# Sparse-attention mixers on one Trainium2 core: both key groups of a tile side by side, with two front banks and one selected bank

## What is computed

```python
p_cmp = masked_softmax(einsum('bghsd,bngd->bghsn', qh, k_cmp), cmp_mask)     # compressed keys
o_cmp = einsum('bghsn,bngd->bghsd', p_cmp, v_cmp)
imp = einsum('bghsn,nj->bgsj', p_cmp, overlap)                               # importance of 32 blocks of 64 keys
sel_score = where(eligible, imp + FORCE_BONUS * forced, -1.0)
_, sel_idx = lax.top_k(sel_score, 8)                                         # 8 blocks for the selected branch
o_slc = softmax over the keys of the selected blocks, times their values
o_win = softmax over the last 256 keys, times their values
o = gates[0] * o_cmp + gates[1] * o_slc + gates[2] * o_win
```

## Time and profile before

| | |
|---|---|
| median of 3 runs | 3451.02 us (3449.68 to 3454.45) |
| profiled execution | 3451.55 us, its span 3449.6 us |
| mean granted TensorE clock | 0.954 |
| TensorE / VectorE / ScalarE / GpSimd busy | 93% / 42% / 29% / 31% of the span |
| first step of the mixers to last turn | 698.2 to 1766.8 us |

### The profile page before, as it was taken

How to read it: one execution, slowest core, us unless ns; L and a number is a source line. 1 busy time by engine, 2 the same in 40 slices (tenths; PEclk the granted TensorE clock), 3 DMA queues, 4 the chain that set the end, 5 groups by cost and what they waited for, 6 DMA issues and landing times. The chain is left out here.

```text
span 3449.6 us, 42933 instructions
## 1 busy us (share of the span) xinstructions
PE 3202.7 (93%) x15500; PEld 2516.8 (73%) x15500; DVE 1435.8 (42%) x2615; ACT 998.3 (29%) x1652; POOL 1078.3 (31%) x615
## 2 busy tenths in 40 slices
PE   7999998667888999999979969999999999999999
PEld 7999998644555555555548758888888878888887
DVE  3113111046656666665532133335433533354333
ACT  3012000033434444444430032232222322232221
POOL 3222221043423223222010044444344444444442
PEclk9999999658889999999999979999999999999999
DMA  5223222210101001000023342223322232333321
GB/s 172 97 96 101 97 96 81 67 55 32 64 32 64 33 32 64 32 32 7 13 105 134 117 157 94 93 94 130 102 97 97 95 126 96 97 98 122 97 97 61
DMA packets 164983, 291.21 MB, mean 84 GB/s; under 512 B 19167, under 2 KB 126559, under 8 KB 162780
## 3 DMA queue, kind: packets, MB, share of 16 engines
q1 hardware_dynamic: 160252, 272.79, 23.4%
q10 hardware_dynamic: 4608, 16.78, 1.4%
HBM read 239.01 MB, written 50.53 MB: 84 GB/s over the span
## 5 line engine op out<-in xcount | busy, mean ns | idle before, releaser
L1752 POOL TENSOR_TENSOR mlp_down_lo<-mlp_down_raw,mlp_down_hi 128x2048 fp32r<-128x2048 f32 x64 | 298.5, 4663 | 750.5 <-ACT mlp_down_hi L1791 750.5
L1872 DVE TENSOR_TENSOR mlp_y<-mlp_acc,mlp_y 128x512 f32<-128x512 f32 x512 | 344.5, 688 | 201.4 <-PE mlp_acc L1950 196.5
L1950 PE MATMUL mlp_acc<-mlp_down_hi,mlp_f_hi 128*128 128x512 f32 x1024 | 402.6, 393 | 10.6 <-DVE mlp_y L1872 10.6
L1928 PE MATMUL mlp_up<-mlp_hT_hi,mlp_up_hi 128*128 128x512 f32 x1024 | 399.6, 390 | 2.5 <-DVE mlp_hT_lo L1894 2.5
L1950 PE MATMUL mlp_acc<-mlp_down_hi,mlp_f_lo 128*128 128x512 f32 x1024 | 400.2, 391 | 0.0
L1950 PE MATMUL mlp_acc<-mlp_down_lo,mlp_f_hi 128*128 128x512 f32 x1024 | 400.1, 391 | 0.0
L1928 PE MATMUL mlp_up<-mlp_hT_hi,mlp_up_lo 128*128 128x512 f32 x1024 | 399.4, 390 | 0.0
L1928 PE MATMUL mlp_up<-mlp_hT_lo,mlp_up_hi 128*128 128x512 f32 x1024 | 399.3, 390 | 0.0
L1859 DVE TENSOR_TENSOR mlp_f<-mlp_relu 128x512 f32<-128x512 f32 x128 | 134.4, 1051 | 601.8 <-ACT mlp_relu L1798 601.8
L311 PE MATMUL proj_acc<-proj_w_hi,proj_hT_hi 128*128 128x344 f32 x1152 | 369.9, 321 | 10.9 <-issue 9.8
L311 PE MATMUL proj_acc<-proj_w_hi,proj_hT_lo 128*128 128x344 f32 x1152 | 367.9, 319 | 0.0
(11 more groups left out here) (251 smaller groups left out, 5427.0 us busy)
## 6 DMA issues: line engine op xcount, KB each, us to landing
mlp_up_raw<-in_w_up SPq DMA_DIRECT2D x64, 1024.0 KB, 5.2
mlp_down_raw<-in_w_down SPq DMA_DIRECT2D x64, 1024.0 KB, 4.8
proj_w_raw<-in_w_in SPq DMA_DIRECT2D x18, 1376.0 KB, 6.4
z_scratch<-proj_z_out SPq DMA_DIRECT2D x144, 172.0 KB, 1.9
mix_z<-z_scratch SPq DMA_DIRECT2D x16, 1548.0 KB, 6.9
proj_x_tile<-in_x ACTq DMA_DIRECT2D x16, 512.0 KB, 3.9
mixed_scratch<-mix_mixed SPq DMA_DIRECT2D x16, 512.0 KB, 2.9
out_mixed<-mixed_scratch SPq DMA_DIRECT2D x16, 512.0 KB, 4.1
```

The source lines that it names most:

```text
L1752: nc.gpsimd.tensor_tensor(dn_lo[:, b, :, :], dn_raw[:, :, :], dn_hi[:, b, :, :].bitcast(F32), ALU.subtract).then_inc(dn_lo_done, 1)
L1872: nc.vector.tensor_tensor(y[:, yb, tt, cols], acc[i % AR][:, :], y[:, yb, tt, cols], ALU.add).then_inc(added, 1)
L1928: mm = nc.tensor.matmul(up_ps[t % 2][:, :], w[:, b, k, cols], h[:, k, :], start=k == 0 and w is up_hi and h is h_hi, stop=k == KT - 1 and ...
L1950: mm = nc.tensor.matmul(acc[i % AR][:, :], a[:, b, k, tt * P:(tt + 1) * P], w[:, b, k, c * BANK:(c + 1) * BANK], start=k == 0 and a is f_h ...
```

## The change

`Plan` orders by tiles instead of by units. `front` of both groups of a tile, each followed by its own select and selected maxima, become one list, `pair(i)`: group 1 follows four steps (`LAG`) behind group 0, the steps alternating. The own work of both groups of tile i is one list too and is merged with `pair(i + 1)`, itself merged with the whole prep of tile i+2. The front bank is now two, one per group, and everything of a front that was one buffer (maxima, negated maxima, weights, sums, selection) is two; the selected bank is one, so the first "values" of a unit waits until the unit before has been lifted, turned and read by its "post". Eight banks are used before and after. No instruction's shape or count in the mixers changes, except that GpSimd clears a selection buffer of twice the size once.

```diff
@@ Plan
+LAG = 4
-        first = self.front(0) + self.select(0) + self.front(1) + self.selected_maxima(0)
-        self.steps = self.prep(0) + merge(first, self.prep(1))
-        for u in range(units):
-            i, g = divmod(u, GROUPS)
-            own = [("scores", u, SLC, 0)]
-            for j in range(1, i + 1):
-                own += [("scores", u, SLC, j), ("values", u, SLC, j - 1)]
+        self.steps = self.prep(0) + merge(self.pair(0), self.prep(1))
+        for i in range(tiles):
+            own = self.own(GROUPS * i) + self.own(GROUPS * i + 1)
             ahead = []
-            if u + 2 < units:
-                pieces = self.prep(i + 2) if i + 2 < tiles else []
-                half = len(pieces) // GROUPS
-                ahead = merge(self.front(u + 2), pieces[g * half:(g + 1) * half])
-            self.steps += own[:1]
-            if u >= 1:
-                self.steps.append(("turn", u - 1, SLC))
-            if u + 1 < units:
-                self.steps += self.select(u + 1)
-                ahead = merge(self.selected_maxima(u + 1), ahead)
-            if u >= 1:
-                self.steps.append(("post", u - 1, SLC))
-            self.steps += own[1:5] + merge(own[5:] + [("values", u, SLC, i), ("lift", u, SLC)], ahead)
-        self.steps += [("turn", units - 1, SLC), ("post", units - 1, SLC)]
+            if i + 1 < tiles:
+                ahead = merge(self.pair(i + 1), self.prep(i + 2) if i + 2 < tiles else [])
+            self.steps += merge(own, ahead)
...
+    def own(self, u):
+        tiles = list(self.key_tiles(u, SLC))
+        steps = [("scores", u, SLC, tiles[0])]
+        if u % GROUPS:
+            steps.append(("turn", u - 1, SLC))
+        steps += [("scores", u, SLC, j) for j in tiles[1:2]]
+        if u % GROUPS:
+            steps.append(("post", u - 1, SLC))
+        for j in tiles:
+            steps.append(("values", u, SLC, j))
+            steps += [("scores", u, SLC, k) for k in tiles[j + 2:j + 3]]
+        steps.append(("lift", u, SLC))
+        return steps + ([("turn", u, SLC), ("post", u, SLC)] if u % GROUPS else [])
+    def pair(self, i):
+        a, b = (self.front(u) + self.select(u) + self.selected_maxima(u) for u in (GROUPS * i, GROUPS * i + 1))
+        return a[:LAG] + [step for two in zip(a[LAG:], b) for step in two] + b[len(a) - LAG:]
@@ mixers_phase: buffers
-        selected_ps = [m.ps(f"selected{b}", [P, BANK]) for b in range(2)]
-        front_ps = m.ps("front", [P, BANK])
+        selected_ps = m.ps("selected", [P, BANK])
+        front_ps = [m.ps(f"front{b}", [P, BANK]) for b in range(2)]
@@ PE, "compressed": the front bank's wait
-                    if u >= 1:
-                        pe.wait_ge(rows_set, u)
+                    if u >= 2:
+                        pe.wait_ge(rows_set, u - 1)
@@ PE, "values": the selected bank's wait
-                        if branch == SLC and u >= 2:
-                            pe.wait_ge(selected_read, u - 1)
+                        if branch == SLC and u >= 1:
+                            pe.wait_ge(selected_read, u)
```

More of the change, by code:

```diff
@@ L720, in __init__ @@
                 self.values_n[s[1:]] = len(self.values_n)
+            elif s[0] == "post" and s[2] != SLC:
+                self.front_n[s[1:]] = len(self.front_n)
         self.probs_by = list(self.probs_n)
@@ L839, in mixers_phase @@
         chosen = m.sb("chosen", [P, NBLK])
-        selection = m.sb("selection", [P, P])
+        selection = m.sb("selection", [P, 2, P])
         weighted = m.sb("weighted", [P, HPG, HEAD])
@@ L950, in _ @@
             link(nc.gpsimd.memset(state[:, :, :], 0.0))
-            nc.gpsimd.memset(selection[:, :], 0.0).then_inc(cleared, 1)
+            nc.gpsimd.memset(selection[:, :, :], 0.0).then_inc(cleared, 1)
             pool.wait_ge(cleared, 1)
@@ L1086, in _ @@
                         act.wait_ge(turn_sum[branch], u)
-                    bank = selected_ps[u % 2] if branch == SLC else front_ps
+                    bank = selected_ps if branch == SLC else front_ps[u % 2]
                     nc.scalar.copy(lifted[branch][0:VROWS, :], bank[0:VROWS, :]).then_inc(lift_done[branch], 1)
@@ L1118, in maxima_done @@
             def maxima_done(u, branch):
-                if u >= 1:
-                    dve.wait_ge(score_sum, plan.scores_n[u - 1, branch, "row"] + 1)
-                nc.vector.tensor_scalar(neg_max[:, branch, :], top[:, branch, :], MASKED / 10, -1.0,
+                if u >= 2:
+                    dve.wait_ge(score_sum, plan.scores_n[u - 2, branch, "row"] + 1)
+                nc.vector.tensor_scalar(neg_max[:, u % 2, branch, :], top[:, u % 2, branch, :], MASKED / 10, -1.0,
                                         ALU.max, ALU.mult).then_inc(max_ready[branch], 1)
@@ L1227, in _ @@
                         dve.wait_ge(turn_sum[branch], u + 1)
-                    out = (selected_ps[u % 2] if branch == SLC else front_ps)[:, 0:HPG * VCOLS[branch]]\
+                    out = (selected_ps if branch == SLC else front_ps[u % 2])[:, 0:HPG * VCOLS[branch]]\
                         .rearrange("p (h c) -> p h c", h=HPG)
@@ L1261, in _ @@
                     else:
-                        read, count = (selected_read, u + 1) if branch == SLC else (front_read, 2 * u + 2)
+                        read, count = (selected_read, u + 1) if branch == SLC else (front_read, plan.front_n[u, WIN] + 1)
                         link(nc.vector.scalar_tensor_tensor(out=den[:, 1, :], in0=out[:, :, HEAD], scalar=1e-30,
@@ L1371, in _ @@
                         mm = nc.tensor.transpose(score_ps[n % 2][0:1, h * P:(h + 1) * P],
-                                                 neg_max[:, branch, h:h + 1], ident[:, :])
+                                                 neg_max[:, u % 2, branch, h:h + 1], ident[:, :])
                     mm.then_inc(score_sum, 1)
@@ L1417, in _ @@
                     if branch == CMP:
-                        out = front_ps[:, 0:HPG * VCOLS[CMP]].rearrange("p (h c) -> p h c", h=HPG)
+                        out = front_ps[u % 2][:, 0:HPG * VCOLS[CMP]].rearrange("p (h c) -> p h c", h=HPG)
                         for h in range(HPG):
```

62 lines of the change are left out of this document (32 added, 30 removed).

## The result

The changed kernel takes 3513.5 us (median of 4 runs, 3511.0 to 3518.7) against 3450.4 us of the kernel before in the same runs: ratio 1.0182, 95% interval 1.0165 to 1.0200. It is 63 us slower; the forecast was 48 us faster, 3403 us, in a range of 3352 to 3440. The profiled execution has a span of 3510.7 us.

The account below looks back on a forecast made before the run. The prediction took PE (TensorE, 93% busy) to bound the kernel, losing 90 us idle in the mixers plus half-clock time. Terms -23 - 20 - 10 - 15 + 15 + 5 = -48 us from 3451.02 gave 3403 us, range 3352 to 3440.

Parts of the forecast that it names:

- The selected row: Selected scores waiting for their row: about ten rows now stand between, so 23 of 24.0 us go.
- The window branch's tail: Waits of window turn and window value products, 25.9 us: the other group's steps cover them, 20 us saved.
- Window rows, select, compressed: Their 14.6 us of PE waits: second front bank and other chain cover them, 10 us saved.
- The clock: PE's half clock follows its idling, so less idling returns speed: 15 us saved, bounds 0 and 34.
- The second group's row: Selected row directly after its last maximum, 1.24 us in sixteen tiles: costs 15 us, at most 19.8.
- Maxima side by side: Both groups' selected maxima in one run at a tile's end, VectorE slower than PE's row: costs 5 us.
- One selected bank: A unit's first value product waits for the unit before; other steps cover it: 0, bound 62 us.
- three signs: Forecast wrong if maxima waits pass 15 us, first value products regularly wait over 1, or tiles 1-8 shorten by 55.
- B: Rival, 20%: covered waits return as waits on VectorE, smaller gain, around 3431 to 3440 us; sign: maxima waits past 15.
- D: Rival, 7%: uncovered single selected bank costs 62 us, +14, 3465 us; sign: first value products regularly wait over 1 us.
- A: Rival, 22%: cover and clock feed each other, -86, 3365 us; sign: tiles 1 to 8 end 55 us shorter or more.

Follow-up runs that it names:

- e14: The changed kernel with only the window row one step later in the front, behind the compressed values: 3496.5 us, ratio 1.0143.
- e13: e6 with the window row one step later in the front, behind the compressed values: 3379.8 us, ratio 0.9792.
- e3: The changed kernel with the second group's selected row moved from the pair's end into the first group's own steps: 3501.1 us, ratio 1.0149.
- e6: The changed kernel with the moves of e1 and e3 together: 3406.5 us, ratio 0.9881.
- e7: The changed kernel's banks, buffers and waits with the order of steps of the kernel before: 3504.2 us, ratio 1.0161.
- e1: The changed kernel with the prep piece "output sums" four pieces sooner in the list: 3437.0 us, ratio 0.9955.
- e2: The kernel before with "output sums" moved as in e1: 3447.8 us, ratio 1.0001.
- e10: The changed kernel with the first product of GpSimd's rotation done twice in each tile: 3533.1 us, ratio 1.0240.
- e11: e1 with the first product of GpSimd's rotation done twice in each tile: 3446.6 us, ratio 0.9986.

## Why the prediction was wrong

*The selected row (-23).* Right: 0.2 us of 24.0 are left. (The 9.8 us of it in the late tiles are 70% of the 14.1 us idle there, not "nearly all"; no term rests on that.)

*The window branch's tail (-20).* Right in size: 4.8 of 25.9 us are left, 21 gone.

*Window rows, select, compressed (-10).* Wrong for the rows. "The other chain covers window rows" failed: the waits of window rows for the negated maximum grew from 1.8 us to 19.9. e14 moved window rows alone and took 17.6 us off the waits for negated maxima. The other chain doesn't only stand between, it also puts its own work into VectorE's queue ahead of the reduction that the row needs (the timeline at 836 to 842 us). Select fell from 3.6 us to 0.8 and compressed from 2.8 to nothing, but the handoff they belong to came back as the 6.6 us that the selected maxima wait for the selection's rows.

*The clock (-15).* The sign turned with the idle time. It was 0.90 and 0.96 in tiles 1 to 15, and 18 of the 63 us are PE's longer busy time. In e13 the clock came back, 1.00 through tiles 1 to 15, with 51 us of busy time at the lower level where the kernel before has 112.

*The second group's row (+15).* They wait 22.1 us in the changed kernel, 1.38 each. Moving these rows took 19.2 us off the waits (e3), 31 us off the time with GpSimd out of the way (e6), 12 with it in the way. The mechanism was right, the size a little small.

*Maxima side by side (+5).* Right in size: waits for the reductions are 6.1 us.

*One selected bank (0, bound 62).* Right in the order by tiles: value products of the selected branch wait 0.7 us in the changed kernel. The bound was no exaggeration: in the old order, where one unit's turn and post stand just ahead of the next unit's values, it costs 55 us (e7), 33 of them the wait itself. For that order the rule of the Trainium skill that the prediction weighed (Perfetto Trace Analysis, section Matmuls) is what happens; in the new one the steps of the pair cover it.

*What was missing: GpSimd.* The step that failed is the sentence that everything is in what stands between the two ends of a handoff, because I then walked only handoffs of PE, ScalarE and VectorE, and called prep steps "cover". Prep is itself a chain, with GpSimd in it. The old list put half a prep into each unit and five own steps, a turn and a select ahead of each half; the new one starts the next prep a few steps behind the last piece of the one before. GpSimd needs 9.3 us between the two, from "output sums" to the rotated keys. It cost 76 us (e1), more than the whole loss, and was neither in a term, nor in a rival, nor in the range. e2, e10 and e1 together show it: nothing in the old order, longer when GpSimd's work is longer, gone when its release comes sooner. With it out of the way the kernel takes 3437 us: faster than before and inside the forecast's range, but 34 us above 3403. Rows still wait 52.0 us for the negated maximum there, where the prediction counted 15 to 20.

None of the three signs that were to tell the forecast wrong came as it was put: waits for VectorE's reductions of maxima stayed at 6.1 us (B; the negated maxima, with 46.3, were the place to look), the first value product of a unit hardly waited (D), and tiles 1 to 8 grew longer (A). All three look at PE's waits for known partners, and GpSimd was not one.

Of the rivals, D ends on the right side, but its mechanism isn't what made the changed kernel slower. A's 3365 is nearly reached by e13, 3380, but only after three moves that the change doesn't make. Its rule in the Trainium skill (TensorE: Matmul & The Clock Gate, section What's actually happening) is that activity lifts the half rate. e13's tiles 1 to 8 agree: PE busy 94%, clock 1.00. The busy share alone doesn't tell the clock, though: tiles 9 to 15 of the changed kernel are busy 94% too, at 0.96. B, waits that go over to VectorE, is true of 18 us of window rows.

The sum by time: taken alone from the changed kernel, the three moves give 76 (e1), 12 (e3) and 17 us (e14), 105 together; all three give 134 (e13). The 29 us between say that each move is worth more once the others are made; how much of that is uncovered waits and how much the clock was not measured apart. From the changed kernel to e13 PE's idle time falls by 85 us and its busy time by 46.

Open: why the waits in e10 grew by more than the time added; by which chain e11 loses its 10 us; what decides when the clock falls; and the price of the single selected bank in the new order by itself, since a second one would need a ninth bank and wasn't tried.

## What to carry to other kernels

When one list orders several engines, walk it once for every engine that takes part, the slow one at the side as well, and write down for each chain how much time it has between its release and its next use; a change of order is also a change of when each chain is released. A step that covers a wait on one engine lengthens the queue on another, so cover must be counted on the engine that is waited for. Where waits stand in series on an in-order engine, a move that shortens one may only lengthen the next, so judge it again when the next one is gone: the same move gave 12 us with GpSimd's wait in place and 31 without.

## What was unexpected of the hardware

A small chain on GpSimd is long: thirteen operations on 4 to 512 columns took 9.3 us, 1.02 us of them for a power on four columns and 1.27 for a product on 512. And idle time of PE can cost more than itself through the clock: 48 us of waits were worth 76, and in e13, with 47 us of PE idle time in these stretches instead of 132, the clock was 1.00 from tile 1 to tile 15. But the two don't move in step: in e10 PE was idle 29 us more and spent 30 us less of its busy time at the lower level. A wait far shorter than that of tile 5 can be followed by a fall too: the one that ends at 1253.8 us lasted 2.1 us, and the lower level began at 1255.2.
